# Three low-part buffers of their own for the seven-product up quarters, begun a pair ahead, and renamed banks

## What is computed

```python
D_MODEL = 1024
D_FF = 4 * D_MODEL
DEPTH = 2
...
    for i in range(DEPTH):
        ...
        hdn = rmsnorm(x, p["norm_mlp"][i]) @ p["w_up"][i]
        x = x + (jnp.square(jax.nn.relu(hdn)) @ p["w_down"][i]).astype(x.dtype)
```

## Time and profile before

| what | value |
|---|---|
| median of 3 runs | 2512.14 us (2508.95 to 2515.58) |
| the profiled execution | 2513.55 us, span 2511.8 us |
| TensorE busy | 2422.0 us (96%) |
| VectorE busy | 1217.9 us (48%) |
| ScalarE busy | 1121.6 us (45%) |
| GpSimd busy | 424.3 us (17%) |
| mean granted TensorE clock | 0.989 |

### The profile page before, as it was taken

The page is one execution under the profiler, slowest core; times in us unless marked ns, Lnnn a source line. Parts: engine busy times, 40 slices in busy tenths (PEclk is TensorE's granted clock), DMA queues, the critical chain, the costliest instruction groups (busy, mean ns, idle before and its releaser), DMA issues.

```text
span 2511.8 us, 33003 instructions
## 1 busy us (share of the span) xinstructions
PE 2422.0 (96%) x12972; PEld 2075.1 (83%) x12972; DVE 1217.9 (48%) x1861; ACT 1121.6 (45%) x2127; POOL 424.3 (17%) x488
## 2 busy tenths in 40 slices
PE   8999999999999899999999999999999998999996
PEld 6888678887888888888888885888878888988885
DVE  7877674104326433425378777630143255243354
ACT  5544536434445343435435435454344444344353
POOL 1111002320122121111112110123102211212120
PEclk9999999999999999999999999999999999999998
DMA  5554317862456454555555553379616564646554
GB/s 161 104 101 109 95 59 166 185 140 55 99 119 122 109 121 107 125 122 105 105 114 114 102 109 92 85 163 185 125 26 127 121 138 89 126 100 128 118 112 117
DMA packets 116325, 289.12 MB, mean 115 GB/s; under 512 B 13190, under 2 KB 13574, under 8 KB 116180
## 3 DMA queue, kind: packets, MB, share of 16 engines
q0 software_dynamic: 69696, 126.91, 30.2%
q1 hardware_dynamic: 46484, 160.20, 22.6%
HBM read 283.91 MB, written 3.15 MB: 114 GB/s over the span
## 4 chain that ended last, share of the span: by engine, by line
PE 88%; DMA 6%; DVE 3%; ACT 1%; issue 1%; DVEq 0%; SPq 0%; POOL 0%
PE G L989 57%; DMA wlo<-wstream 6%; PE M L1208 2%; PE M L1441 2%; PE M L1443 2%; PE M L1442 2%; PE G L1441 2%; PE G L1390 2%; PE M L946 2%; PE G L1443 2%; PE G L1442 2%; PE M L957 1%; PE M L959 1%; PE M L958 1%; PE G L1221 1%
## 5 line engine op out<-in xcount | busy, mean ns | idle before, releaser
L477 POOL DMA_DIRECT2D wlo<-wstream x408 | 358.3, 879 | 1528.6 <-ACT wlo L518 1450.7
L518 ACT ACTIVATE wlo<-raw 128x512 fp32r<-128x512 f32 x388 | 244.2, 629 | 755.6 <-PE G L989 667.8
L989 PE MATMUL G<-B_lo,whi 128*128 128x256 f32 (+1 forms) x1536 | 521.3, 339 | 0.0
L989 PE MATMUL G<-B_hi,whi 128*128 128x256 f32 (+1 forms) x1536 | 488.3, 340 | 0.2 <-issue 0.2
L989 PE MATMUL G<-B_hi,wlo 128*128 128x256 f32 (+1 forms) x1536 | 388.9, 334 | 0.0
L989 PE MATMUL G<-A_lo,whi 128*128 128x256 f32 x1120 | 382.1, 341 | 0.0
L989 PE MATMUL G<-A_hi,whi 128*128 128x256 f32 x1120 | 363.1, 346 | 15.3 <-DVE A_lo L1535 8.2
L989 PEld LDWEIGHTS G<-B_hi,wlo 128*128 128x128 f32 x1536 | 288.6, 188 | 69.3
L989 PEld LDWEIGHTS G<-B_lo,whi 128*128 128x128 f32 x1536 | 290.4, 189 | 31.5 <-issue 0.5
L1506 DVE TENSOR_TENSOR X<-X,G 128x768 f32<-128x768 f32 x94 | 89.6, 953 | 434.6 <-PE G L989 307.1
L989 PEld LDWEIGHTS G<-B_hi,whi 128*128 128x128 f32 x1536 | 290.3, 189 | 1.2 <-issue 0.5
(11 more groups left out here) (374 smaller groups left out, 3845.8 us busy)
## 6 DMA issues: line engine op xcount, KB each, us to landing
raw<-wstream SPq DMA_DIRECT2D x234, 512.0 KB, 4.0
wlo<-wstream POOLq DMA_DIRECT2D x456, 256.0 KB, 5.3
raw_b<-wstream SPq DMA_DIRECT2D x24, 512.0 KB, 7.0
ring<-dft SPq DMA_DIRECT2D x12, 512.0 KB, 3.3
w_low<-wstream POOLq DMA_DIRECT2D x24, 256.0 KB, 6.3
mraw<-memT SPq DMA_DIRECT2D x16, 256.0 KB, 3.4
X<-xT SPq DMA_DIRECT2D x8, 384.0 KB, 7.5
win<-dft SPq DMA_DIRECT2D x6, 512.0 KB, 4.8
```

What stands on the lines that cost most here:

```text
L477: pool.dma_start(low, wstream[stream(L, c)][:, part], accum_op=ALU.add).then_inc(lo_in[c % 2][h], 16)
L518: act.activation(wlo[:, s, part], raw[:, s, part], ACT.Copy, scale=-1.0).then_inc(neg_done, 1)
L989: last = mm(out, w, p[:, k, a:b], start=(k == 0 and w is w_hi and p is parts[0]), stop=(k == KT - 1 and w is w_lo))
```

## The change

Three buffers w_low[0..2] take the low parts of n = 0, 4 and 6. Two lie one behind the other over wdt2 and rbc (4096 bytes together), the third over dt_ and what follows it. One helper `pair_neg(q, p, i)` makes the three negations, for pair p + 1 behind products 1, 5 and 6 of pair p, and for pair 0 in the last two tiles of the down stage before (two in tile 6, one in tile 7). `pair_low(p, i)` issues the three DMAs of a pair in turn. wlo then holds only VectorE's low parts. In the banks of a pair 1 and 2 change places, and the first product of a stage waits for the last down tile but one; the last one is waited for at n = 2.

```diff
--- before.py
+++ after.py
@@ -139,14 +139,15 @@
 
         cst = small("cst", [P, NCONST])
         par = small("par", [P, NPAR])
+        o_low = at[0]
         wdt2 = small("wdt2", [P, KT, 2, 16], F32R)
-        o_rbc = at[0]
         rbc = small("rbc", [P, T])
         acc = small("acc", [P, T + 6])
         sq = small("sq", [P, T + 6])
         rmem_bc = small("rmem_bc", [P, M2])
         stat = small("stat", [P, 4, 8])
         rcol, rmem = small("rcol", [P, 8]), small("rmem", [P, 4])
+        o_dt = at[0]
         dt_, dA, cum, ecum, wst, dec = (small(n, [P, 2, TT, HEADS]) for n in
                                         ("dt_", "dA", "cum", "ecum", "wst", "dec"))
         negA = small("negA", [P, 16])
@@ -225,7 +226,7 @@
         raw_b = place("raw_b", [P, 2, D], oE + 36864)
         assert oE + 36864 + 8192 <= 229344
         p_one, p_five, v_sum = acc[:, 0:HALF_T], acc[:, HALF_T:T], sq[:, 0:HALF_T]
-        w_low = place("w_low", [P, 512], o_rbc, F32R)
+        w_low = [place(f"w_low{i}", [P, 512], o, F32R) for i, o in enumerate((o_low, o_low + 2048, o_dt))]
         h_buf = [sq[:, HALF_T:T], rmem_bc[:, 0:HALF_T]]
 
         def pair_raw(p):
@@ -325,7 +326,8 @@
         out_r = sem("out_ready")
         c_src, c_hi, c_lo = sem("combination_ready"), sem("combination_hi"), sem("combination_lo")
         raw_b_in = [sem(f"raw_b_in{i}") for i in range(2)]
-        u_mm, u_hi, u_neg, u_neg1, u_dlo = (sem(n) for n in ("fast_product", "fast_hi", "fast_neg", "fast_first_neg", "fast_lo"))
+        u_mm, u_hi, u_dlo = (sem(n) for n in ("fast_product", "fast_hi", "fast_lo"))
+        u_neg = [sem(f"fast_neg{i}") for i in range(3)]
         u_lo = [sem(f"fast_low_in{i}") for i in range(3)]
         u_s = sem("weight_sums")
         u_p1, u_p5, u_v, u_u1, u_c = sem("p1_copied"), sem("p5_copied"), sem("p5_p7_added"), sem("p1_p6_added"), sem("fast_sum")
@@ -483,24 +485,16 @@
                 for q in range(1, QUARTERS):
                     U, w = (L * FAST + q - 1) * 4, L * STREAM + C_MLP + 16 * q
 
-                    def first_low(p):
-
-                        pool.wait_ge(u_neg1, U + p + 1)
-                        pool.dma_start(w_low[:, :], wstream[w + 2 * p][:, 0:512], accum_op=ALU.add).then_inc(u_lo[0], 16)
-
-                    def later_low(p, i):
-
-                        s, part = part_of(7 * p + (4, 6)[i])
-                        pool.wait_ge(u_neg, 2 * (U + p) + i + 1)
-                        pool.dma_start(wlo[:, s, part], wstream[w + 2 * p + i][:, 512:1024],
-                                       accum_op=ALU.add).then_inc(u_lo[1 + i], 16)
-
-                    first_low(0)
+                    def pair_low(p, i):
+
+                        row, col = ((0, 0), (0, 1), (1, 1))[i]
+                        pool.wait_ge(u_neg[i], U + p + 1)
+                        pool.dma_start(w_low[i][:, :], wstream[w + 2 * p + row][:, col * 512:(col + 1) * 512],
+                                       accum_op=ALU.add).then_inc(u_lo[i], 16)
+
                     for p in range(4):
-                        later_low(p, 0)
-                        if p < 3:
-                            first_low(p + 1)
-                        later_low(p, 1)
+                        for i in range(3):
+                            pair_low(p, i)
                     for m in range(8):
                         low_halves(L, C_MLP + 8 + 8 * q + m)
 
@@ -814,11 +808,12 @@
                         return raw_in, L * LOADS + (C_MLP + 16) // 2 + 6 * (q - 1) + p // 2
                     return raw_b_in, (L * FAST + q - 1) * 2 + p // 2
 
-                def first_neg(q, p):
+                def pair_neg(q, p, i):
 
                     arrived, k = arrival(q, p)
-                    act.wait_ge(arrived[0], 16 * (k + 1))
-                    act.activation(w_low[:, :], quad(p, 0, 0), ACT.Copy, scale=-1.0).then_inc(u_neg1, 1)
+                    row, col = ((0, 0), (0, 1), (1, 1))[i]
+                    act.wait_ge(arrived[row], 16 * (k + 1))
+                    act.activation(w_low[i][:, :], quad(p, row, col), ACT.Copy, scale=-1.0).then_inc(u_neg[i], 1)
 
                 def weight_high(q, j):
 
@@ -831,8 +826,6 @@
                     if n in (1, 2, 3, 5):
                         act.wait_ge(u_s, 4 * U + (2, 1, 3, None, 4)[n - 1])
                     src = quad(p, *((0, 0), (1, 0), (0, 0), (0, 0), (0, 1), (0, 0), (1, 1))[n])
-                    if n in (4, 6):
-                        act.activation(wlo[:, s, part], src, ACT.Copy, scale=-1.0).then_inc(u_neg, 1)
                     act.activation(whi[:, s, part], src, ACT.Copy).then_inc(u_hi, 1)
 
                 def fast_up(q):
@@ -850,13 +843,13 @@
                                 act.wait_ge(raw_in[s], 16 * (L * LOADS + (C_MLP + 16) // 2 + 6 * (q - 1) + 2 + 1))
                             act.activation(wlo[:, s, part], raw[:, s, part], ACT.Copy, scale=-1.0).then_inc(neg_done, 1)
                             act.activation(whi[:, s, part], raw[:, s, part], ACT.Copy).then_inc(hi_done, 1)
-                        if n == 1 and i < 21:
-                            first_neg(q, i // 7 + 1)
+                        if n in (1, 5, 6) and i < 21:
+                            pair_neg(q, i // 7 + 1, n // 3 if n < 6 else 2)
                         if n == 0:
                             act.wait_ge(u_c, 3 * U + 1)
                             act.activation(p_one, bank[0][:, 0:HALF_T], ACT.Copy).then_inc(u_p1, 1)
                         if n == 1:
-                            act.activation(p_five, bank[2][:, 0:HALF_T], ACT.Copy).then_inc(u_p5, 1)
+                            act.activation(p_five, bank[1][:, 0:HALF_T], ACT.Copy).then_inc(u_p5, 1)
                         if n == 4:
                             act.activation(h_buf[1], bank[0][:, 0:HALF_T], ACT.Relu).then_inc(u_c11, 1)
                             act.wait_ge(u_c11, U + 1)
@@ -884,8 +877,8 @@
                             act.wait_ge(raw_in[s], 16 * (L * LOADS + first + (m + 2) // 2 + 1))
                             split(s, c + m)
                         else:
-                            if m == 6:
-                                first_neg(q + 1, 0)
+                            for i in ((0, 1), (2,))[m - 6]:
+                                pair_neg(q + 1, 0, i)
                             for h in range(2):
                                 act.wait_ge((half_used, chunk_used)[h], c + m + 1)
                                 weight_high(q + 1, 2 * s + h)
@@ -1417,12 +1410,14 @@
                     U0 = (L * FAST + q - 1) * 4
                     for p in range(4):
                         U, bank = U0 + p, (GB, MB)[p % 2]
-                        for n, (src, b) in enumerate(((B11, 0), (T1, 2), (T3, 3), (T2, 1), (B21, 0), (B22, 2), (T4, 3))):
+                        for n, (src, b) in enumerate(((B11, 0), (T1, 1), (T3, 3), (T2, 2), (B21, 0), (B22, 1), (T4, 3))):
                             j = 7 * p + n
                             s, part = part_of(j)
                             if p == 0 and n == 0:
+                                pe.wait_ge(psum_free, L * TILES + T_MLP + 16 + 8 * (q - 1) + 1)
+                                pe.wait_ge(c_lo, 28 * (L + 1))
+                            if p == 0 and n == 2:
                                 pe.wait_ge(psum_free, L * TILES + T_MLP + 16 + 8 * (q - 1) + 2)
-                                pe.wait_ge(c_lo, 28 * (L + 1))
                             if p >= 2 and n < 4:
                                 pe.wait_ge(*((u_c11, U - 1), (u_c, 3 * U - 3), (u_c, 3 * U - 2), (u_u1, U - 1))[n])
                             if n >= 4:
@@ -1436,8 +1431,8 @@
                             for k in range(4):
                                 w = part.start + k * P
                                 w_hi, w_lo = whi[:, s, w:w + P], wlo[:, s, w:w + P]
-                                if n == 0:
-                                    w_lo = w_low[:, k * P:(k + 1) * P]
+                                if n in (0, 4, 6):
+                                    w_lo = w_low[n // 3][:, k * P:(k + 1) * P]
                                 mm(out, w_hi, src[0][:, k, :], start=(n < 4 and k == 0), stop=False, skip_group_check=n > 3)
                                 mm(out, w_hi, src[1][:, k, :], start=False, stop=False, skip_group_check=n > 3)
                                 last = mm(out, w_lo, src[0][:, k, :], start=False, stop=(k == 3), skip_group_check=n > 3)
@@ -1966,7 +1961,7 @@
                     if n == 1:
                         arrived, k = (raw_in, L * LOADS + (C_MLP + 16) // 2 + 6 * (q - 1) + p // 2) if p % 2 == 0 else \
                             (raw_b_in, (L * FAST + q - 1) * 2 + p // 2)
-                        dve.wait_ge(u_neg1, U + p + 1)
+                        dve.wait_ge(u_neg[0], U + p + 1)
                         dve.wait_ge(u_hi, 7 * (U + p) + 1)
                         dve.wait_ge(arrived[1], 16 * (k + 1))
```

(4 more changed lines are left out.)

## The result

The changed kernel takes **2452.63 us** (median of 4 runs, 2452.21 to 2453.84), the kernel before beside it 2511.97 us: a ratio of 0.9764, 95% interval 0.9747 to 0.9781, or 59.3 us less. The profiled execution is one of 2453.84 us with a span of 2452.1, 59.7 us under that of before. Run again later it came to 0.9781 (0.9767 to 0.9794).

The account below looks back on a forecast made before the run. TensorE bounds the kernel (busy 96% of the span), so only its standing or slow time can be won: 44.5 + 11.5 + 7.3 - 4.2 = 59.1 us off 2513.55, forecast 2454 us, range 2448 to 2472.

Parts of the forecast that it names:

- The waits: Up stages, before n=6 of pairs 0 to 2: all 18 TensorE waits on late low parts go, 44.5 us gained.
- the clock: Up stages: the eight stretches of TensorE at half clock go, 11.5 us gained, 1.4 us each.
- the price of a wait beyond its idle time: TensorE, each wait: costs 0.16 us more than its idle time, 2.9 us for 18 waits.
- a stage's undisturbed length: Up stage with nothing late: 59.97 us, TensorE's busy time in the second stage, which had full clock throughout.
- The start: Start of each up stage: n=0 no longer waits for the last down tile's addition to X, 7.3 us gained.
- No cost on ACT, POOL and at the stage's end: Moved negations fit ACT's idle time, POOL's new order and the down quarter's first low half lose nothing: cost 0.
- The new wait: Before n=0 of pair 2 in each stage: its low part lands 0.7 us late, 4.2 us lost in six.
- its chain: VectorE and ACT feed each other from L2011's start to L1984's end, 12.7 us, while five products take 10.6.
- one such wait gives pair 3 its slack: Up stages: the wait before n=0 comes before pair 2 only, 0.7 us late, six times.
- The estimate from the Trainium skill: A 256 KB GpSimd DMA takes 2.6 us; n=0's low part would be 4 us early, whole gain 63.3 us.
- slot 0 in time: Rival, before n=0: its low part lands in 6.1 to 6.6 us, nothing is lost, 2450 us; chance 0.15.
- The slow clock: Rival, up stages: the eight half-clock stretches stay, 11.5 us, giving 2466 us; chance 0.09.

Follow-up runs that it names:

- renamed banks alone: The kernel before with only the renamed banks and the earlier first product of a stage, low parts as before: 2504.32 us, ratio 0.9959.
- late start: The change with its three buffers and banks, but low parts of n=4 and n=6 negated as late as before, POOL's order as before: 2503.02 us, 0.9958.
- the repeated execution: The change itself, unaltered, run and profiled again on another occasion: 2453.23 us, ratio 0.9781 to the kernel before.
- the held loads: The change with a pair's raw loads issued only once the low part of n=0 of the pair before has landed: 2445.66 us, ratio 0.9753.
- the sooner slot 0: The change with the low part of n=0 negated behind product 0 of the pair before instead of product 1: 2446.03 us, ratio 0.9729.
- n=6 alone: The change with the low part of n=4 back in wlo, negated behind product 0 of its own pair; n=0 and n=6 early: 2485.94 us, 0.9914.

## Why the prediction was right

The forecast was 2454 us, 59.1 us off the profiled execution; it was 59.7.

- **The waits** (44.5 us) and **the clock** (11.5 us), together 56.0: a stage with nothing late is 59.05 us, so they were worth 411.99 - 354.3 = 57.7 us. The mechanism is right; the term that was too small is the price of a wait beyond its idle time, taken as 0.16 us. It is 0.21 to 0.26 us in the five stages of the change that have just one delay (60.29 - 1.01 - 59.05 = 0.23, for instance). The part left out stands in the rows above: the second matmul comes 0.25 us behind the first (868.63, 868.88) and not 0.18. The same holds at a stage's start before the change (the second matmul at 840.39, 0.10 us late), and the second stage, with three waits and no low stretch, agrees: (66.64 - 6.83 - 0.10 - 59.05) / 3 = 0.22. For these two reasons a stage's undisturbed length came out 0.28 us too long. With 0.23 the 18 waits were worth 41.6 + 4.1 = 45.7 us, the six starts 0.6 more than their own term says, and 11.4 us are left for the clock, 1.4 us for each low stretch, as forecast. Waits of about the same length had eight low stretches behind them (before), five (renamed banks alone), and seven (late start, two of them in one piece).
- **The start** (7.3 us): measured 7.3 up to the first matmul, and the six waits come back as 6.3 us when the banks do.
- **No cost on ACT, POOL and at the stage's end**: the negations found their room (ACT still idles 0.39 us between them, above), and no down stage starts late.
- **The new wait** (4.2 us): right in its place, its chain (12.7 us as forecast) and its cause, but mis-sized. It cost 359.88 - 354.3 = 5.6 us, and 7.8 us in the repeated execution. The forecast has TensorE start 0.7 us late six times; it started 0.65 + 0.16 = 0.8 us late in the mean, each time with the slower second matmul behind it, and a seventh delay came before pair 3 of the first stage, 0.16 us and so without idle time. The forecast's step that one such wait gives pair 3 its slack therefore holds only in part; in the repeated execution four of the six waits stand before pair 3. Inside the stages that makes 57.7 - 5.6 = 52.1 against 56.0 - 4.2 = 51.8 forecast: two errors of 1.7 and 1.4 us cancel, and that the total came within 0.6 us is luck to this extent. In one stage of six the wait comes before pair 3 (at 1138.55, 1.01 us) and not before pair 2, for which slot 0 had landed in 5.2 us. The estimate from the Trainium skill (DMA: Bandwidth & Descriptors, Anatomy of one DMA), 2.6 us, is not borne out: the shortest landing at L492 was 3.6 us, and this transfer's with no loads beside it 4.0. (The forecast's "under 3.6 us" is of the up stages' transfers; over the whole kernel before one of the same size and kind, at L477, took 3.5.)
- **The rivals**: slot 0 in time (2450 us) did not come, but the held loads and the sooner slot 0 show it was one edit away, and worth 5.6 to 7.8 us. The slow clock did not stay: none of the six waits had a low stretch behind it, nor had the six of the repeated execution.

What the prediction left out: the clock falls outside the up stages too, in the profile of before at 69.3 and 1308.4 (3.41 us each) and from 2492.78 to the end, in that of the change at 26.3 and 2432.69 (3.41 us each) and from 2439.52 to the end. What these stretches were worth is not known; all that lies outside the stages and their starts differs by 59.7 - 59.4 = 0.3 us.

The forecast for n=6 alone (2467 us, measured 2486) failed at the step that let one wait per stage serve all later pairs. There the slack that a wait gave lasted for one pair.

## What to carry to other kernels

When a wait repeats at the same place of a loop, look at what lies between releasing its cause and the wait, and move the cause ahead by whole steps, or take away what runs beside its transfer (tested here for slot 0 alone); a buffer of its own is worth only the time that it lets the work start earlier. Then ask which other stage of the pipeline had been living on the slack of that wait: here n=4 (when it was left where it was) and slot 0, neither late before, both became late without it. A transfer that the critical engine will want soon should be issued ahead of the bulk loads and not beside them.

## What the runs showed of the hardware

- A 256 KB adding DMA, the same transfer of the same pair, landed in 4.0 us with the two raw loads of 512 KB held back, in 4.4 us with the first of them 1.4 us behind it, and in 6.9 us with both starting within 1.07 us of it. The low part of n=6 in the kernel before landed in 7.2 to 8.4 us 18 times with raw loads (and the low part of n=0) beside it, and in 3.6 to 5.1 us six times without.
- A wait of TensorE cost 0.21 to 0.26 us more than the idle time that the profile shows: 0.16 before the first matmul and 0.07 before the second.
- A missing cover shows late: the waits before n=6 had been hiding two producers. TensorE then waited 2.0 to 3.1 us for n=4 in pair 1 (when it had no early start) and 0.2 to 1.0 us for slot 0, once 2.4 us in the repeated execution.
- A wait of some 2 us was not always followed by a fall of the clock. Over the kernel before and five others here, 84 waits of 1.5 us or more in the up stages had 28 stretches at half clock (3.41 us each, one of 6.83) begin within 1.5 us of their end (some just before it), from 2 behind 17 waits in one kernel to 7 behind 12 in another; none of the waits up to 1.32 us had one. No run tells which waits are followed by one. At 1.4 us each, two against eight such stretches are 8 us. The medians of the kernel before went from 2507.65 to 2515.04 us, and single runs from 2503.85 to 2519.11; the changed kernel's, whose profiled stages have no such stretch, still went from 2449.34 to 2456.22.
